# Unread products in TensorE's gaps, and the list of further passes made inside expert 0

## The chip, the cores and the metric

One Trainium2 chip, one core of it. The metric is the device time of one execution in microseconds (us), lower is better. TensorE is called PE below, VectorE DVE, ScalarE ACT, GpSimd POOL and SyncE SP.

## What is computed

One layer of a hybrid decoder trunk over 256 tokens of width 1024, in fp32. The last two thirds of it matter here: after the mixing sublayer a LayerNorm, a router that gives each token 4 of 32 experts, and the experts.

```python
x = layer_norm(ALPHA * x + mix, ln1_g, ln1_b)
logits = x @ w_router + b_router                 # (256, 32)
top_vals, top_idx = lax.top_k(logits, 4)         # gates = softmax(top_vals)
for e in range(32):
    g, u = split(x @ w_gate_up[e] + b_gate_up[e])    # 1024 -> 2 x 1024
    act = (clip(u, -7, 7) + 1) * (min(g, 7) * sigmoid(1.702 * min(g, 7)))
    out += combine[:, e] * (act @ w_down[e] + b_down[e])
h = ALPHA * x + out
x = layer_norm(h + sigmoid(h @ w_pg) * (p @ w_pp), ln2_g, ln2_b)
```

The kernel doesn't run every expert on every token. It gathers the tokens that chose the expert, up to 64 in a pass.

## The kernel before

The program writes out an order of instructions for each engine by hand, with semaphores between them (`wait_ge` before a step, `then_inc` behind it). There is no planner.

**Front** (to about 220 us). All weights come through one queue of transfers that SP issues, and PE takes the input projections, the attention, the convolution branch and the products of `mix` (L784 to L793).

**Between mix and the experts.** The residual is made in quarters on DVE (`residual`), turned on PE (`turn_res`, L795), copied out by ACT (`turned`), and multiplied with the router's weights on PE (`route`, L804). DVE picks the four experts of each token in `pick` (L1519 to L1537), which leaves a mask in `mask`, and raises `mask_ready` once for each half of the tokens. PE makes running counts with three small products (L832 to L834) and sums with twelve-odd tiny instructions (L837, L840). DVE forms each token's slot (L1561) and the one-hot matrix of experts 0 and 1 (`one_hot`, L461, `sel_ready`). PE gathers the rows of both experts with it: `gather` (L369 to L379), 16 products in two halves of 8, each two instructions of 128 columns, into banks 0 and 1. ACT copies each half out (L499).

**The list of further passes.** Behind the gather PE ranks the pairs of expert and pass that hold more than 128 tokens (L848, written to bank 7), DVE makes `place` from it (L1588), PE turns that into a list and its length (L850, L851), and DVE copies the list to integers (L1595, `more_out`). Only after this does PE wait for `wide_ready`, read the flag of expert 0 from SBUF into a register (`read_flag`, L511; the flag says if an expert has over 64 tokens) and branch on it. An expert with the flag 0 runs `one_round`, one with the flag 1 runs `two_rounds`. Here one expert, number 14, runs two rounds.

**one_round(e)** on PE (L962 to L987): turn the gates (L382), 32 products of the gathered rows with the gate and up weights (L388, 64 instructions), then turn the two sums (L395) once ACT has copied them (L1234). In expert 0 the first turning waits for `more_out`. Then the bias rows are turned (L944, expert 0 only), the expert before is combined (L408), in odd experts the next pair is gathered, and the down products follow (`use_down`, L388 again), which wait for `t_read`, raised by DVE's second addition at L434. DVE's part is `swiglu` (L428 to L452), ACT's the sigmoid (L457).

**Where the branches lie.** On PE the code of `one_round` follows in line and that of `two_rounds` stands behind everything. On ACT and DVE it is the other way: both wait for `wide_ready`, read the flag, and branch to `act_experts` or `dve_experts` past the code of all 32 `two_rounds` and of the further passes. On ACT this comes behind L499, on DVE behind L1595. DVE then reads the flag of the next expert before each `swiglu`.

**Weights.** Each expert takes 12 MB in six transfers of 2 MB. There are eleven slots for them. SP waits until a slot has been read (`chunk_used`, `gu_done`, `d_done`) before it issues the next transfer (L336 by the profile).

```python
                pe.wait_ge(more_ready, 1)                      # L847
                pe.matmul(bank[7][0:MORE, 1:2], upper[0:MORE, 0:MORE], need, ...).then_inc(rank_done, 1)
                pe.wait_ge(more_ready, 2)
                pe.matmul(bank[6][0:1, 3 * NE:3 * NE + LIST], expert_no, place, ...)
```

Of the kernel before, what the change touches and what calls it, by code (L numbers as in the profile page):

```python
# [7 lines left out]
D, S, P = 1024, 256, 128  # L8
# [21 lines left out]
NMORE = (S - WIDE) // CAP  # L30
MORE = NMORE * NE
LIST = NT * P * TOPE // CAP


Q0, K0, V0, QI0 = 0, 512, 1024, 1536
# [44 lines left out]
def program(nc, x, xT, pT, w_in, bT, bki, b_in, w_oa, w_oc, w_out, dwT, convT, ln1T, ln1g, ln1b, w_r, b_r,  # L80
# [4 lines left out]
    with ctx:  # L85
# [280 lines left out]
        def gate_bank(t, j):  # L366
            return bank[4 * t + j][:, 0:256]

        def gather(pe, b=4, first=False):  # L369

            for k in range(KD):
                if first and k % 4 == 0:
                    pe.wait_ge(x1_ready, 3 + k // 4)
                for t in range(NT):
                    mm = pe.matmul(bank[b + k // 4][:, (k % 4) * P:(k % 4 + 1) * P], x1_rows[:, t, k // 2, k % 2, :],  # L375
                                   sel[:, t, :, :], start=(t == 0), stop=(t == NT - 1))
                if k % 4 == 3:
                    mm.then_inc(gath_done, 1)
# [126 lines left out]
        def read_flag(eng, flag, e):  # L505
            if e == 1:
                eng.wait_ge(more_out, 1)
            eng.reg_load(flag, wide[0:1, e:e + 1] if e < NE else more[0:1, LIST:LIST + 1])

        with nc.Block() as block:  # L510
# [121 lines left out]
            def _(pe):  # L632
# [151 lines left out]
                def mix(t, j, ks=range(KD)):  # L784
                    for k in ks:
                        if t == 0 and k == 0:
                            wait_chunk(pe, 25 + j)
                        if t == 0 and j == 0:
                            pe.wait_ge(merged_ready, k + 1)
                        mm = pe.matmul(mix_bank(t, j), merged[:, k, t * P:(t + 1) * P], w_view(25 + j)[:, k, :],  # L790
                                       start=(k == 0), stop=(k == KD - 1))
                    if k == KD - 1 and (t == 1 or j == 3):
                        mm.then_inc(mix_done, 1)  # L793

                def turn_res(t, j):  # L795
                    pe.wait_ge(res_ready, 4 * t + j + 1)
                    if t == 1:
                        pe.wait_ge(rt_out, 3 + j)
                    for k in range(2):
                        mm = pe.transpose(turn_bank(t, j)[:, k * P:(k + 1) * P],  # L800
                                          res[:, t, (2 * j + k) * P:(2 * j + k + 1) * P], ident)
                    mm.then_inc(rt_done, 1)

                def route(t, ks):  # L804
                    for k in ks:
                        if k % 2 == 0:
                            pe.wait_ge(rt_out, 4 * t + k // 2 + 1)
                        mm = pe.matmul(bank[t][:, 0:NE], resT[:, k, t * P:(t + 1) * P], wr_sb[:, k, :],
                                       start=(k == 0), stop=(k == KD - 1))
                    if k == KD - 1:  # L810
                        mm.then_inc(rl_done, 1)
# [12 lines left out]
                turn_res(1, 2)  # L824
                route(1, range(4))
                mix(1, 3, range(4, KD))
                route(1, range(4, 6))
                turn_res(1, 3)
                route(1, range(6, KD))

                pe.wait_ge(mask_ready, 2)
                pe.matmul(bank[6][:, 0:NE], upper, mask[:, 0, 0:NE], start=True, stop=True)  # L832
# [5 lines left out]
                for j in range(NMORE):  # L838
                    for t in range(NT):
                        mm = pe.matmul(bank[7][j * NE:(j + 1) * NE, 0:1], mask[:, t, 0:NE], ones[:, 0:1],  # L840
                                       start=(t == 0), stop=(t == NT - 1))
                mm.then_inc(cum_done, 1)

                pe.wait_ge(sel_ready, 1)
                gather(pe, 0, True)

                pe.wait_ge(more_ready, 1)  # L847
                pe.matmul(bank[7][0:MORE, 1:2], upper[0:MORE, 0:MORE], need, start=True, stop=True).then_inc(rank_done, 1)  # L848
                pe.wait_ge(more_ready, 2)
                pe.matmul(bank[6][0:1, 3 * NE:3 * NE + LIST], expert_no, place, start=True, stop=True)  # L850
                pe.matmul(bank[6][0:1, 3 * NE + LIST:3 * NE + LIST + 1], need, ones[0:MORE, 0:1], start=True, stop=True  # L851
                          ).then_inc(list_done, 1)

                top = nc.cur_bb
                flag = pe.alloc_register("pe_two_rounds")

                def pair(n):
                    pe.wait_ge(e_in[slot_no[n]], filled[n])  # L860
# [102 lines left out]
                def one_round(e):  # L963
                    q = e % 2
                    weights = lambda c: pair(load_no(e, c))
                    turn_gates(pe, selg[:, q]).then_inc(sgt_done, 3)
                    embedded(e)
                    use_gate_up(e, q, weights, e == 0)
                    for j, (rows, to) in enumerate(((h_gate, gate_turned), (h_up, up_turned))):
                        pe.wait_ge(h_out, 4 * e + 1 + j)  # L970
                        if j:
                            pe.wait_ge(g2_out, 3 * e + 3)
                        elif e:
                            pe.wait_ge(rows_out, 2 * e)
                        else:
                            pe.wait_ge(more_out, 1)
                        turn(pe, rows, to).then_inc(t_done, 1 + 2 * j)
                    read_flag(pe, flag, e + 1)
                    if e == 0:
                        turn_bias(gate_sum)  # L980
                    before(e)
                    if q == 1 and e < NE - 1:
                        next_gather(e)
                    if e in (PP_E, PP_E + 2):
                        embed(e)
                    use_down(e, weights)

                def two_rounds(e):
                    q = e % 2
                    weights = lambda c: pair(load_no(e, c))  # L990
                    turn_gates(pe, selg[:, q]).then_inc(sgt_done, 1)
                    embedded(e)
                    if e == 0:
                        pe.wait_ge(more_out, 1)
                        turn_bias(gate_turned)
                        pe.wait_ge(xt_ready, 1)
                    pe.wait_ge(selb_ready, 3 * e + 1)
                    for k in range(KD):
                        for t in range(NT):
                            mm = pe.matmul(gate_sum[:, k * CAP:(k + 1) * CAP], x1_rows[:, t, k // 2, k % 2, :],  # L1000
                                           sel_b[:, t, :], start=(t == 0), stop=(t == NT - 1))
                    mm.then_inc(sgt_done, 1)
                    pe.wait_ge(g2_out, 3 * e + 2)
                    if e:
                        pe.wait_ge(rows_out, 2 * e)
                    else:
                        pe.wait_ge(bias_ready, 1)
                    use_gate_up_twice(e, q, weights)
                    read_flag(pe, flag, e + 1)
                    before(e)  # L1010
                    for j, (rows, to) in enumerate(((h_gate, gate_sum), (h_up, up_sum))):
                        pe.wait_ge(h_out, 4 * e + 1 + j)
                        turn(pe, rows, to).then_inc(t_done, 1)
                    for j, (rows, to) in enumerate(((h_gate, gate_turned), (h_up, up_turned))):
                        pe.wait_ge(h_out, 4 * e + 3 + j)
                        turn(pe, rows, to).then_inc(t_done, 1)
                    pe.wait_ge(t_read, 2 * e + 1)
                    pe.wait_ge(selb_ready, 3 * e + 3)
                    for t in range(NT):
                        mm = pe.transpose(gate_sum[:, t * P:(t + 1) * P],  # L1020
                                          selg[:, q, t].rearrange("p h c -> p (h c)"), ident)
                    mm.then_inc(sgt_done, 1)
                    if q == 1 and e < NE - 1:
                        pe.wait_ge(g2_out, 3 * e + 3)
                        next_gather(e)
                    use_down_twice(e, weights)
                    pe.wait_ge(rows_out, 2 * e + 1)
                    pe.wait_ge(g2_out, 3 * e + 3)
                    combine(pe, 1 - q).then_inc(d_done, 1)
                    if e in (PP_E, PP_E + 2):  # L1030
                        embed(e)

                pe.wait_ge(wide_ready, 2)
                read_flag(pe, flag, 0)
                for e in range(NE):
                    if e % 2 == 0:
                        if e:
# [294 lines left out]
            def _(v):  # L1332
# [227 lines left out]
                for t in range(NT):  # L1560
# [24 lines left out]
                gates_by_slot(v, 0, 1)  # L1585
                v.wait_ge(more_ready, 1)
                v.wait_ge(rank_done, 1)
                nc.vector.tensor_scalar(place, iota_e[0:MORE, 0:LIST], bank[7][0:MORE, 1:2], need, ALU.is_equal, ALU.mult  # L1588
                                        ).then_inc(more_ready, 1)
                v.wait_ge(zeroed, 1)  # L1590
                nc.vector.tensor_copy(gate_rows.rearrange("p t (h c) -> p t h c", h=2)[:, :, :, 0:NE],
# [135 lines left out]
```

## Time and profile before

| | |
|---|---|
| time, median of 3 runs | 1195.64 us (1194.48 to 1196.38) |
| the profiled execution: time, span | 1196.13 us, 1194.4 us |
| PE, DVE, ACT busy | 97%, 25%, 14% |
| DMA, mean over the span | 375 GB/s, 448.16 MB |

The span is what the profiler saw, and the time has 1.7 us around it. "Busy" counts an engine's data instructions alone. PE instructions overlap, so a group's busy time is shorter than its count times the duration of one. PEclk is the clock that TensorE was granted: 1.00 is 2.4 GHz, 0.50 is 1.2 GHz. Durations of weight loads (PEld) lie beside the products.

### The profile page before, as it was taken

Reading aid. Unit: us, or ns where it says so; the run is one execution under the profiler, and the core shown is the slowest. Engines: PE = TensorE matmul, PEld = TensorE weight load, DVE = VectorE, ACT = ScalarE, POOL = GpSimd, SP = SyncE. Lnnn points to the kernel's source line nnn. Section 1 sums busy time; section 2 is a strip of 40 time slices with the busy share of each in tenths; the row PEclk is TensorE's granted clock in tenths of the full one; section 3 lists DMA queues with packets and bytes.
Section 4 is the critical chain, followed back from the end, with each engine's and each line's share of the span. In section 5 each row is a group of like instructions: output and inputs, shape, how many; then the busy total and the mean of one; then the engine's idle time right before and its main releaser. Section 6 shows DMA issues by size and latency. Waiting matters only on the chain.

```text
span 1194.4 us, 13688 instructions
## 1 busy us (share of the span) xinstructions
PE 1153.3 (97%) x5606; PEld 580.7 (49%) x5606; DVE 297.1 (25%) x769; ACT 172.5 (14%) x335; POOL 11.5 (1%) x26
## 2 busy tenths in 40 slices
PE   7999999899999999999999799999999999999997
PEld 6888888834343434434343343434343343434346
DVE  0549932611111121111110211111112111111125
ACT  1204130111010111101010111101111111111112
POOL 0020000000000000000000000000000000000000
PEclk9999999899999999999998899999999999999999
DMA  9994466779999999999999999999999999999980
GB/s 324 346 292 141 141 254 239 276 325 426 427 427 427 428 427 427 428 426 428 428 424 427 395 364 421 427 429 427 428 427 426 430 426 427 425 428 428 428 347 36
DMA packets 64887, 448.16 MB, mean 375 GB/s; under 512 B 7120, under 2 KB 36080, under 8 KB 39984
## 3 DMA queue, kind: packets, MB, share of 16 engines
q1 hardware_dynamic: 58352, 440.84, 89.7%
q10 hardware_dynamic: 6464, 6.33, 1.6%
q8 instruction: 49, 0.80, 0.3%
q14 instruction: 22, 0.18, 0.0%
HBM read 444.53 MB, written 2.62 MB: 374 GB/s over the span
## 4 chain that ended last, share of the span: by engine, by line
PE 89%; DVE 4%; DMA 4%; ACT 1%; issue 1%; ACTq 0%; DVEq 0%
PE bank L388 56%; PE bank L648 11%; PE bank L375 5%; DMA ring<-in_w_gu 3%; PE bank L408 3%; PE bank L777 2%; PE bank L790 2%; PE bank L1066 2%; PE bank L395 2%; PE bank L703 1%; DVE arena L434 1%; PE bank L382 1%; DVE arena L428 1%; ACT arena L1234 1%; DVE arena L452 1%
## 5 line engine op out<-in xcount | busy, mean ns | idle before, releaser
L388 PE MATMUL bank<-ring,arena 128*64 128x512 f32 x1712 | 379.2, 597 | 9.8 <-issue 5.2
L388 PE MATMUL bank<-arena 128*64 128x512 f32 x1456 | 322.9, 597 | 4.6 <-DVE arena L434 3.9
L388 PEld LDWEIGHTS bank<-ring,arena 128*64 128x64 f32 x1712 | 120.6, 137 | 246.3 <-issue 231.9
L388 PEld LDWEIGHTS bank<-arena 128*64 128x64 f32 x1456 | 102.1, 138 | 207.8 <-issue 194.1
L428 DVE TENSOR_TENSOR arena<-bank,arena 128x512 f32<-128x512 f32 x33 | 22.8, 692 | 614.1 <-PE bank L395 614.1
L648 PE MATMUL bank<-arena,ring 128*128 128x256 f32 x576 | 129.0, 385 | 0.0
L648 PEld LDWEIGHTS bank<-arena,ring 128*128 128x128 f32 x576 | 110.6, 193 | 17.4 <-issue 2.2
L1234 ACT ACTIVATE arena<-bank 128x512 f32<-128x512 f32 x62 | 37.1, 598 | 396.2 <-PE bank L388 396.2
L408 PE MATMUL bank<-arena 64*128 64x512 f32 x272 | 67.6, 615 | 2.0 <-ACT arena L1237 1.4
L375 PEld LDWEIGHTS bank<-sel,arena 128*128 128x128 f32 x512 | 63.5, 202 | 11.8 <-issue 11.4
L375 PE MATMUL bank<-sel,arena 128*128 128x128 f32 x512 | 66.6, 290 | 0.3 <-DVE sel L461 0.3
L1237 ACT ACTIVATE arena<-bank 128x512 f32<-128x512 f32 x33 | 19.7, 597 | 249.5 <-PE bank L388 247.4
L395 PEld LDWEIGHTS bank<-arena 128*128 128x128 f32 x264 | 36.7, 209 | 35.0 <-issue 25.9
L395 PE MATMUL bank<-arena 128*128 128x128 f32 x264 | 48.8, 309 | 3.1 <-ACT arena L1234 0.4
L1420 DVE SCALAR_TENSOR_TENSOR arena<-arena 128x256 f32<-128x256 f32 x120 | 48.5, 477 | 0.7 <-DVE arena L1420 0.2
L408 PEld LDWEIGHTS bank<-arena 64*128 64x128 f32 x272 | 23.5, 186 | 24.4 <-issue 17.5
L461 DVE TENSOR_TENSOR sel<-arena 128x256 f32<-128x256 f32 x16 | 6.8, 425 | 108.9 <-PE bank L382 108.8
L1132 ACT ACTIVATE arena<-bank,arena 128x256 f32<-128x256 f32 x36 | 16.8, 473 | 103.0 <-PE bank L648 103.0
L452 DVE TENSOR_TENSOR arena<-arena 128x256 f32<-128x256 f32 x66 | 28.1, 425 | 5.0 <-ACT arena L457 1.1
L499 ACT ACTIVATE arena<-bank 128x512 f32<-128x512 f32 x32 | 19.1, 597 | 70.2 <-PE bank L375 70.2
L448 DVE SCALAR_TENSOR_TENSOR arena<-arena 128x256 f32<-128x256 f32 x66 | 28.0, 425 | 4.2 <-DVE arena L444 0.3
L790 PE MATMUL bank<-ring,arena 128*128 128x256 f32 x128 | 28.4, 380 | 0.0
(196 smaller groups left out, 529.7 us busy)
## 6 DMA issues: line engine op xcount, KB each, us to landing
ring<-in_w_gu SPq DMA_DIRECT2D x70, 2048.0 KB, 25.7
arena<-in_w_gu SPq DMA_DIRECT2D x58, 2048.0 KB, 27.2
ring<-in_w_dn SPq DMA_DIRECT2D x35, 2048.0 KB, 25.0
arena<-in_w_dn SPq DMA_DIRECT2D x29, 2048.0 KB, 26.6
ring<-in_w_in SPq DMA_DIRECT2D x19, 1024.0 KB, 12.6
ring<-in_w_out SPq DMA_DIRECT2D x4, 1024.0 KB, 5.6
arena<-in_w_pg SPq DMA_DIRECT2D x2, 2048.0 KB, 44.2
ring<-in_w_oa SPq DMA_DIRECT2D x2, 1024.0 KB, 5.7
```

The lines of the kernel that those rows point to most:

```text
L375: mm = pe.matmul(bank[b + k // 4][:, (k % 4) * P:(k % 4 + 1) * P], x1_rows[:, t, k // 2, k % 2, :], sel[:, t, :, :], start=(t == 0), stop= ...
L388: mm = pe.matmul(to[half * CAP:(half + 1) * CAP, :], rows, w[:, half * 512:(half + 1) * 512], start=first, stop=last)
L395: mm = pe.transpose(to[:, j * P:(j + 1) * P], blocks[:, j, :], ident)
L408: mm = pe.matmul(total[t][n][:, :], G2[a:a + CAP, q, t * P:(t + 1) * P], ysb[a:a + CAP, :], start=first, stop=last)
L428: nc.vector.tensor_tensor(by_bias(gt, 8), by_bias(of_gate[:, :], 8), bias_of(e, 0, 0, 8), ALU.add).then_inc(sw_step, 1)
L448: nc.vector.scalar_tensor_tensor(up[:, at], up[:, at], 1.0, gt[:, at], ALU.add, ALU.mult).then_inc(sw_step, 1 + 6 * skip * j)
L452: nc.vector.tensor_tensor(to[:, at], up[:, at], sg[:, at], ALU.mult).then_inc(act_ready, 1 + 2 * skip * j)
L648: mm = pe.matmul(bank[n % 4][:, 0:S], w[:, k, j * P:(j + 1) * P], xT_sb[:, k, :], start=(k == 0), stop=(k == KD - 1))
L777: mm = pe.matmul(bank[n % 4][:, 0:S], w_view(i)[:, k, (c % 4) * P:(c % 4 + 1) * P], rhs[:, k, :], start=(k == 0), stop=(k == 3))
L790: mm = pe.matmul(mix_bank(t, j), merged[:, k, t * P:(t + 1) * P], w_view(25 + j)[:, k, :], start=(k == 0), stop=(k == KD - 1))
L1234: a.activation(rows, of[:, :], ACT.Identity).then_inc(h_out, 1 + 2 * j)
L1420: nc.vector.scalar_tensor_tensor(cy[:, a, :], u_sb[:, a, bass.ds(j, S)], dw[:, a, bass.ds(j, 1)], cy[:, a, :], ALU.mult, ALU.add).then_inc ...
```

## The change

Five unread products of 256 columns (`keep_clock`) are put where PE waits: one behind the last turning of the residual, three behind the last route product, one behind the counts. They write bank 0, which the gather overwrites. The gather is split in two, and the wait for `wide_ready` and the reading of expert 0's flag go between the halves. The rank product writes bank 6 in place of bank 7. The two list products leave the place ahead of expert 0 and follow the gate and up products of expert 0 (the copy at L1595 so follows there too, and the turning behind them still waits for it). The wait and flag reading ahead of the loop over the experts go.

```diff
+RANK = 3 * NE + LIST + 1
@@ gather
-        def gather(pe, b=4, first=False):
-            for k in range(KD):
+        def gather(pe, b=4, first=False, ks=range(KD)):
+            for k in ks:
@@ tensor, between mix and the gather
+                def keep_clock(n):
+                    for _ in range(n):
+                        pe.matmul(bank[0][:, 0:S], ident, resT[:, 0, :], start=True, stop=True)
                 route(1, range(4, 6))
                 turn_res(1, 3)
+                keep_clock(1)
                 route(1, range(6, KD))
+                pe.wait_ge(mask_ready, 1)
+                keep_clock(3)
 
                 pe.wait_ge(mask_ready, 2)
                 pe.matmul(bank[6][:, 0:NE], upper, mask[:, 0, 0:NE], start=True, stop=True)
...
                 mm.then_inc(cum_done, 1)
+                keep_clock(1)
 
                 pe.wait_ge(sel_ready, 1)
-                gather(pe, 0, True)
-
+                gather(pe, 0, True, range(4))
+                flag = pe.alloc_register("pe_two_rounds")
+                pe.wait_ge(wide_ready, 2)
+                read_flag(pe, flag, 0)
+                gather(pe, 0, True, range(4, KD))
                 pe.wait_ge(more_ready, 1)
-                pe.matmul(bank[7][0:MORE, 1:2], upper[0:MORE, 0:MORE], need, start=True, stop=True).then_inc(rank_done, 1)
-                pe.wait_ge(more_ready, 2)
-                pe.matmul(bank[6][0:1, 3 * NE:3 * NE + LIST], expert_no, place, start=True, stop=True)
-                pe.matmul(bank[6][0:1, 3 * NE + LIST:3 * NE + LIST + 1], need, ones[0:MORE, 0:1], start=True, stop=True
-                          ).then_inc(list_done, 1)
+                pe.matmul(bank[6][0:MORE, RANK:RANK + 1], upper[0:MORE, 0:MORE], need, start=True, stop=True
+                          ).then_inc(rank_done, 1)
                 top = nc.cur_bb
-                flag = pe.alloc_register("pe_two_rounds")
+                def list_further():
+                    pe.wait_ge(more_ready, 2)
+                    pe.matmul(bank[6][0:1, 3 * NE:3 * NE + LIST], expert_no, place, start=True, stop=True)
+                    pe.matmul(bank[6][0:1, 3 * NE + LIST:3 * NE + LIST + 1], need, ones[0:MORE, 0:1], start=True,
+                              stop=True).then_inc(list_done, 1)
@@ one_round
                     use_gate_up(e, q, weights, e == 0)
+                    if e == 0:
+                        list_further()
@@ two_rounds
                     if e == 0:
+                        list_further()
                         pe.wait_ge(more_out, 1)
@@ ahead of the loop over experts
-                pe.wait_ge(wide_ready, 2)
-                read_flag(pe, flag, 0)
                 for e in range(NE):
@@ vector
-                nc.vector.tensor_scalar(place, iota_e[0:MORE, 0:LIST], bank[7][0:MORE, 1:2], need, ALU.is_equal, ALU.mult
+                nc.vector.tensor_scalar(place, iota_e[0:MORE, 0:LIST], bank[6][0:MORE, RANK:RANK + 1], need, ALU.is_equal, ALU.mult
```

## Rows read from the trace of the kernel before

**Rows 1.** Windows: each stretch, busy time of PE, granted clock, DMA share, GB/s
```profile
234.00:238.00 4.00, 4.00 (x20) 4.00 (x21) 3.06 (x13) 0.41 (x1) 0.81 (x2) 0.50 1.00 426
...
240.00:242.00 2.00, 1.03 (x9) 0.53 (x10) 0.58 (x3) 0.44 (x1) 0.00 (x0) 1.00 0.04 12
...
687.00:689.00 2.00, 1.31 (x7) 0.69 (x8) 0.00 (x0) 0.60 (x1) 0.00 (x0) 1.00 0.77 172
```

**Rows 2.** Waits of PE, 690 to 1194 us: total, times, longest
```profile
PE bank L388 <- DMA ring<-in_w_gu: 0.5, 1, 0.5
```

**Rows 3.** Chain that ended last, 225 to 262 us: start, length, what
```profile
231.44 0.64 PE bank L832 x2
...
232.50 0.44 PE bank L834 x2
...
233.77 6.03 PE bank L375 x32
239.80 0.22 PE bank L848 x2
...
240.46 0.20 PE bank L850 x2
...
240.70 0.51 issue
...
241.64 13.91 PE bank L388 x64
```

**Rows 4.** Timeline, 222 to 241 us: start, busy, engine, line, count, [idle before <-releaser]
```profile
222.88 1.89 PE L790 MATMUL bank<-ring,arena 128*128 128x256 f32 x8
...
225.02 0.98 PE L808 MATMUL bank<-wr_sb,arena 128*128 128x32 f32 x8
...
229.24 0.63 PE L808 MATMUL bank<-wr_sb,arena 128*128 128x32 f32 x4 [0.47 <-ACT arena L1209]
...
235.29 0.28 DVE L1573 CAST wide<-arena 1x32 int32<-1x32 f32 x1
...
240.74 0.17 DVE L1595 CAST more<-bank 1x17 int32<-1x17 f32 x1 [0.20 <-PE bank L851]
```

**Rows 5.** Chain that ended last, a later gather
```profile
285.29 3.97 PE bank L375 x32
```

**Rows 6.** Timeline of expert 0, 253 to 261 us
```profile
256.24 0.69 DVE L428 TENSOR_TENSOR arena<-bank,arena 128x512 f32<-128x512 f32 x1 [15.34 <-PE bank L395]
...
257.81 1.99 PE L408 MATMUL bank<-arena 64*128 64x512 f32 x8 [0.56 <-ACT arena L1245]
...
260.52 5.80 PE L388 MATMUL bank<-ring,arena 128*64 128x512 f32 x26 [0.73 <-DVE arena L434]
```

**Rows 7.** Timeline of ACT, 232 to 262 us, around its branch to the experts
```profile
239.84 0.60 ACT L499 ACTIVATE arena<-bank 128x512 f32<-128x512 f32 x1 [1.66 <-PE bank L375]
243.05 0.38 ACT L1229 ACTIVATE arena<-bank 128x256 f32<-128x256 f32 x1 [2.62 <-issue]
```

**Rows 8.** DMA queues, 240 to 244 us: packets, MB, share of 16 engines
```profile
q14 instruction: 3, 0.02, 2.0%
```

**Rows 9.** Timeline, 596 to 675 us: expert 13's DVE work, then expert 14
```profile
606.45 0.69 DVE L428 TENSOR_TENSOR arena<-bank,arena 128x512 f32<-128x512 f32 x1 [13.21 <-PE bank L395]
...
609.24 0.41 DVE L434 TENSOR_TENSOR arena<-bank,arena 128x256 f32<-128x256 f32 x1
...
620.24 0.60 ACT L1237 ACTIVATE arena<-bank 128x512 f32<-128x512 f32 x1 [6.49 <-PE bank L388]
622.01 0.44 PE L382 MATMUL bank<-arena 128*128 128x128 f32 x2 [1.88 <-issue]
...
625.56 0.38 ACT L1229 ACTIVATE arena<-bank 128x256 f32<-128x256 f32 x1 [4.72 <-issue]
```

**Rows 10.** Windows of PE, expert 14's wait and what follows: clock third from the end
```profile
670.50:671.00 0.50, 0.00 (x0) 0.50 1.08 459
```

**Rows 11.** Timeline of PE, 655 to 695 us: the products behind that wait
```profile
671.00 16.00 PE L388 MATMUL bank<-ring,arena 128*64 128x512 f32 x64 [5.20 <-issue]
```

## The prediction

> **What bounds the kernel now.** I read the granted clock over the span first, then the waits of PE and the share of the DMA engines, then the chain between 225 and 262 us, and last the timelines of ACT and DVE there. The clock is 1.00 but for a few stretches. One of them covers all of 234 to 238 us, where it is 0.50 (1.2 GHz) [rows 1]. Ahead of it PE had only 0.63 us of small router products and then stood idle until 231.44 us [rows 3, 4]. From there on the chain is PE's and DVE's in turn: counts, one-hot, gather, rank, list, flag, first expert [rows 3].
>
> The experts are close to both limits, PE and the transfers. What matters is which clock sets their end. The transfers have no work at 240 to 242 us (share 0.04), because all slots are full, and again they slacken behind expert 14 (0.77 at 687 to 689 us) [rows 1]. Both times PE frees the slots that restart them. Behind that PE waits for a transfer once, 0.5 us [rows 2]. So the end moves with PE's time at expert 14: what PE gains up to the down products of expert 0 arrives at the end in full, and a stream of weights that merely begins earlier gives nothing.
>
> **The parts and their costs.** All times are against the profiled execution, 1196.13 us around a span of 1194.4. That is 0.49 above the median, and I apply the difference to the median of 1195.64.
>
> *Unread products.* A product of 256 columns is two instructions. Eight such instructions take 1.89 us at the full clock [rows 4], so about 0.43 us a product with the pipeline's end taken off. The first falls into the 0.47 us that PE waits for ACT at 229.24 us [rows 4]. Three behind the last router product add 1.3 us from about 229.6 and end near 231.0, before the mask at 231.44 [rows 3]: nothing on the path. Bounds: 0 if they fit, 0.4 us if the last runs over. I take 0. The fifth starts behind the counts and ends about when the one-hot is there, again 0 (up to 0.4). None of them issues a transfer, and no queue but PE's is touched.
>
> *What the clock gives back.* The stretch would look like the one at 222 to 226 us, where small router products alternate with products of 256 columns and the clock stayed at full [rows 4]. The three count products take 0.44 us each at half clock [rows 3], and four router products take 0.98 us at full [rows 4], 0.25 each. The counts end near 232.3 in place of 232.94. DVE has ended its work before them by then, so it takes them up at once: 0.64 us. The gather takes 6.03 us [rows 3] and a later one of the same 32 instructions 3.97 [rows 5]: 2.06 us. Together 2.7; if the clock falls as before, 0, less 0.4 for the fifth product at half clock.
>
> *Flag between the halves.* `wide_ready` comes at 235.57, 1.8 us behind the gather's start [rows 3, 4], and the first half takes 2.0, so the wait is covered. The reading itself has no row of its own. From below it is 0: the same reading stands between L395 and L944 or L408 in expert 0 with no gap. From above it is the 0.51 us of "issue" in front of L382, which holds this reading, a wait and a branch [rows 3]. I take half, 0.25. If it is dear, half of that gap is what is bought with it, so the sum hardly changes.
>
> *Rank, list, flag out of the way.* From the rank product (239.80) to the gates' turning (241.21) are 1.41 us (0.51 of "issue" from 240.70 ends there) [rows 3]. Left are the rank's instructions and a branch, 0.2 and 0.25: 1.0 us gained. The turning needs bank 7 alone, and the rank is now in bank 6, so it doesn't wait for DVE.
>
> Sum at the start of expert 0's products: 2.7 - 0.25 + 1.0 = 3.45 us earlier.
>
> *List inside expert 0.* Its two products follow the last of the 64 instructions, at 255.5 by the times of before (241.64 + 13.91) [rows 3]. L850 began 0.28 us before L1595, which takes 0.17 [rows 3, 4], so `more_out` comes near 255.95 and the gate's turning is up to 0.5 us late. On PE alone 0.3 to 0.5 us would be lost, since the up sum is turned only at 256.28 anyway.
>
> **The new wait.** L1595 is queued on DVE ahead of its flag reading, its branch to the experts, a second flag reading and all of `swiglu`. Before, they had 15.34 us of idle time to hide in [rows 6]. Now the first addition wants to start at 256.2 to 256.8, and L1595 is issued at 255.75. ACT shows what the same sequence costs (wait, reading, branch past 32 two-round blocks): 3.21 us from the start of L499 to the start of L1229, with nothing but "issue" in between [rows 7], and instruction packets in the DMA queues there [rows 8]. That was with the weight queue silent. In expert 14, with the queue full, ACT's far branch took 4.72 us behind L1237, and PE's left 1.88 us of idle time that its backlog didn't cover [rows 9]. Expert 0 has the full queue too. Bounds for DVE from issue to first addition: 0.4 (nothing but readings) and 5.3 (ACT in expert 14, from 620.24). I take 4.3, ACT's quiet 3.2 plus about 1 for the loaded queue and the second reading: first addition at 260.05.
>
> The Trainium skill says in "Runtime: NRT & Kernel Launch", section "Instruction fetch mechanics", that a taken branch beyond the fetched window waits for a transfer of the target page. The trace agrees with it by the 2.62 us and the packets [rows 7, 8].
>
> From DVE's first addition to the end of its second L434, which releases the down products, are 3.20 us where the sigmoid's table is loaded [rows 9]. So the down products start near 263.3, against 260.52 [rows 6]: 2.85 us late. Net gain 3.45 - 2.85 = 0.6 us.
>
> **The rivals.**
>
> *A, the branch is cheap (0.21).* If DVE's readings and branches take under a microsecond, only the 0.3 to 0.5 us of the late turning are lost, and the gain is 3.1: 1192.5. For it: expert to expert the branches leave no gap. Against it: the 2.62 and 4.72 us, both at far targets. The Trainium skill, "Advanced Engine Details and Errata", section "Control Flow Timing", puts a branch at about 51 ns and a compare-and-branch at about 108 ns, which is this rival's case; the sum by it would be A's.
>
> *B, the clock falls all the same (0.14).* The gap of about 0.4 us before the mask and the small counts behind it may be thin enough. Then the 2.7 us stay away, the fifth product runs at half clock into the gather (0.4), and with DVE's 2.85 the sum is -0.4 - 0.25 + 1.0 - 2.85: 2.5 us slower, 1198.1. It decides against the change as soon as DVE's delay exceeds 0.4 us. Against it: the filled stretch has only gaps under half a microsecond.
>
> *C, the clock falls inside expert 0 (0.22).* PE would idle from about 260.1, where L408 ends [rows 6], to 263.3. In expert 14 the clock fell in an idle time of 5.20 us [rows 10, 11], and the 64 instructions behind it took 16.00 in place of 13.91 [rows 3, 11]: 2.1 us. Net 1.5 slower: 1197.1. For it: 3.2 us are twice the gap in which the clock fell at 231 us. Against it: dense products stand directly on both sides.
>
> *D, the products don't fit or the flag's wait stalls the gather (0.05).* Some 0.5 to 1 us off the gain, near 1195.8.
>
> **How the numbers follow.** The forecast, DVE late and both clocks held, has 0.38: 1195.64 - 0.6 = 1195.0. Its own range, with DVE's sequence from 3.2 to 5.3 us, is 1193.8 to 1196.0. A measurement of this kernel tells about 0.2% from no change, 2.4 us, so the bounds are 1193.2 and 1198.0. Faster has nearly all of A and a little of the forecast with a quick branch: 0.22. Slower has most of B and the bad end of C: 0.13. The rest, 0.65, is neither. The range reaches from A's middle to B's lower part: 1192.4 to 1197.8.
>
> **What would show it.** In the changed kernel's profile the clock should be 1.00 through 228 to 240 us, and the first gather some 4.2 us long. L382 should follow the rank product within 0.5 us, with the gates' turning near 237.8. In expert 0 the two list products should stand behind the 64, with L1595 0.3 us later, and DVE's first addition behind an idle time ended by "issue", 4 us after L1595, with instruction packets in between. PE's down products should wait there for DVE's L434 for over 3 us. DVE's addition within a microsecond of L1595 would make the forecast wrong towards A, a clock of 0.50 in either stretch towards B or C. So would any wait of PE for a transfer between experts 0 and 14, since then PE's gain wouldn't reach the end.

## The result and the profile after

The changed kernel takes 1201.07 us (median of 20 runs, 1196.39 to 1203.23) against 1195.89 (20 runs, 1193.89 to 1196.80) for the kernel before: ratio 1.0044, 95% interval 1.0037 to 1.0051, so 5.2 us slower. It lies above the forecast of 1195.0 us and above the range, which ended at 1197.8. The profiled execution has 1199.94 us and a span of 1198.2, 3.8 us over the profile before.

The timeline of the changed kernel from 225 to 268 us, lines left out (line numbers behind L369 move by 1, those of PE's and DVE's late parts by up to 19; L831 are the unread products):

```profile
229.91 1.54 PE L831 MATMUL bank<-arena 128*128 128x256 f32 x6
231.65 0.41 PE L841 MATMUL bank<-arena 128*128 128x32 f32 x2 [0.20 <-DVE arena L1551]
...
232.77 0.70 PE L831 MATMUL bank<-arena 128*128 128x256 f32 x2
...
233.34 2.15 PE L376 MATMUL bank<-sel,arena 128*128 128x128 f32 x16
...
235.73 2.12 PE L376 MATMUL bank<-sel,arena 128*128 128x128 f32 x16 [0.23 <-issue]
...
237.98 0.44 PE L383 MATMUL bank<-arena 128*128 128x128 f32 x2
...
238.35 13.95 PE L389 MATMUL bank<-ring,arena 128*64 128x512 f32 x64
...
252.51 0.16 DVE L1612 CAST more<-bank 1x17 int32<-1x17 f32 x1 [13.92 <-PE bank L872]
...
252.82 1.21 PE L396 MATMUL bank<-arena 128*128 128x128 f32 x8 [0.35 <-DVE more L1612]
...
259.34 0.69 DVE L429 TENSOR_TENSOR arena<-bank,arena 128x512 f32<-128x512 f32 x1 [6.67 <-issue]
...
260.65 1.28 ACT L458 ACT_TABLE_LOAD   x1 [5.99 <-DVE arena L431]
...
263.02 0.42 DVE L435 TENSOR_TENSOR arena<-bank,arena 128x256 f32<-128x256 f32 x1
```

PE's timeline of the changed kernel, 262 to 300 us:

```profile
263.49 9.76 PE L389 MATMUL bank<-ring,arena 128*64 128x512 f32 x32 [6.70 <-DVE arena L435]
273.18 0.44 PE L383 MATMUL bank<-arena 128*128 128x128 f32 x2
```

The same two lines of the kernel before, PE's timeline, 256 to 285 us:

```profile
260.52 7.09 PE L388 MATMUL bank<-ring,arena 128*64 128x512 f32 x32 [0.73 <-DVE arena L434]
267.54 0.44 PE L382 MATMUL bank<-arena 128*128 128x128 f32 x2
```

The first half reads as forecast. The two halves of the gather take 2.15 and 2.12 us where the whole took 6.03 [rows 3], the flag costs 0.23 us between them, and the products of expert 0 start at 238.35 in place of 241.57: 3.2 us earlier (3.45 forecast). The second half is where the time goes. DVE copies the list at 252.51 and adds the first bias at 259.34, with 6.67 us of "issue" in between, PE stands idle for 6.70 us, and the down products start at 263.49, 3.0 us later than before. Then they take 9.76 us in place of 7.09. The windows of the changed kernel (busy time of each engine, granted clock, DMA share, GB/s) say why:

```profile
258.00:260.00 2.00, 0.00 (x0) 0.00 (x0) 0.66 (x1) 0.00 (x0) 0.00 (x0) 1.00 1.02 434
260.00:262.00 2.00, 0.00 (x0) 0.00 (x0) 1.52 (x5) 1.34 (x2) 0.00 (x0) 1.00 0.99 426
262.00:263.50 1.50, 0.01 (x2) 0.01 (x2) 0.79 (x3) 0.57 (x1) 0.00 (x0) 0.53 0.83 344
263.50:266.00 2.50, 2.50 (x6) 0.75 (x8) 1.11 (x3) 0.00 (x0) 0.00 (x0) 0.50 0.09 39
266.00:268.00 2.00, 2.00 (x8) 0.65 (x6) 0.00 (x0) 0.00 (x0) 0.00 (x0) 0.50 0.00 0
268.00:270.00 2.00, 2.00 (x10) 0.56 (x8) 0.00 (x0) 0.00 (x0) 0.00 (x0) 0.77 0.00 0
```

The clock fell to 0.50 (1.2 GHz) behind some five idle microseconds of PE. So expert 1 begins (L383) at 273.18, against 267.54 before: 5.6 us late. The weights also stop for some 6 us (share 0.09 and less from 263.5 to 270 us): SP sends the next ones only when a slot has been read, and the late down products free none before. The later part differs by the clock in expert 14. The changed kernel's timeline there:

```profile
627.73 0.44 PE L383 MATMUL bank<-arena 128*128 128x128 f32 x2 [1.93 <-issue]
628.55 5.35 PE L1019 MATMUL bank<-arena 128*128 128x64 f32 x32 [0.39 <-DVE arena L484]
634.58 29.14 PE L389 MATMUL bank<-arena 128*64 128x512 f32 x128 [0.69 <-ACT arena L1289]
675.13 15.62 PE L389 MATMUL bank<-ring,arena 128*64 128x512 f32 x64 [5.21 <-issue]
```

And the kernel before, PE's timeline, 612 to 700 us:

```profile
622.83 6.20 PE L1000 MATMUL bank<-arena 128*128 128x64 f32 x32 [0.38 <-DVE arena L483]
629.72 29.89 PE L388 MATMUL bank<-arena 128*64 128x512 f32 x128 [0.69 <-ACT arena L1272]
```

The changed kernel's turning is 5.7 us late and the products behind the long wait 4.1 us [rows 9, 11]: the same instructions take 5.35 and 29.14 us where they took 6.20 and 29.89, because more of this thin stretch (small products with short waits) ran at the full clock. That is luck of this one execution. Without its 1.5 us the profiles would differ by 5.3 us and not 3.8, close to the 5.2 of the medians and the 5.6 at the start of expert 1.

### The profile page after: what moved, and what is told of

Same layout as the page of the kernel before. It is cut to its first block, busy times and chain, and to the rows that moved or that the text cites. A ratio compares the mean times of both kernels' runs of the same rounds, so it can differ in the third digit from the quotient of the medians.

```text
span 1198.2 us, 13708 instructions
## 1 busy us (share of the span) xinstructions
PE 1153.2 (96%) x5616; PEld 578.7 (48%) x5616; DVE 297.5 (25%) x769; ACT 172.7 (14%) x335; POOL 11.5 (1%) x26
## 4 chain that ended last, share of the span: by engine, by line
PE 88%; DVE 4%; DMA 4%; issue 2%; ACT 1%; DVEq 0%; ACTq 0%
PE bank L389 56%; PE bank L649 11%; PE bank L376 5%; DMA ring<-in_w_gu 3%; PE bank L409 3%; PE bank L778 2%; PE bank L791 2%; PE bank L1083 2%; PE bank L396 2%; PE bank L704 1%; DVE arena L435 1%; DVE arena L429 1%; PE bank L383 1%; ACT arena L1251 1%; DVE arena L453 1%
```

## The experiments

Unless it says otherwise, each starts from the changed kernel. Ratios are to the kernel before, run on the same chip.

### e1_list_back: the list products ahead of expert 0 again

```diff
-                    if e == 0:
-                        list_further()
...
+                list_further()
                 def pair(n):
```

> The list products go back ahead of expert 0; the unread products, the split gather and the flag between its halves stay. Theory (DVE's flag reading and far branch, uncovered behind the late list copy, are the whole loss): DVE's first addition again has an idle time ended by PE, the clock stays 1.00 to expert 14, and the products of expert 0 start about 2.6 us earlier than before, so the time is 1193.2, 2.7 us under the kernel before. Rival (the unread products or the flag between the halves cost something the profile does not show): at or above 1196. Rival (the early gain does not reach the end): within 0.5 us of before.

1193.61 us, ratio 0.9974 (0.9960 to 0.9988): 3.1 us under before by the ratio. The whole loss is gone with the place of the list. Unread products and split gather cost nothing that shows.

### e2_list_alone: the late list, and nothing else of the change

```diff
-                keep_clock(1)
...
-                pe.wait_ge(mask_ready, 1)
-                keep_clock(3)
...
-                keep_clock(1)
...
-                gather(pe, 0, True, range(4))
-                gather(pe, 0, True, range(4, KD))
+                gather(pe, 0, True)
...
+                pe.wait_ge(wide_ready, 2)
+                read_flag(pe, flag, 0)
                 for e in range(NE):
```

> The list products in expert 0 alone; no unread products, one whole gather, the flag read ahead of the loop as before. Theory: only the rank, list and copy time of about 0.7 us is gained ahead of expert 0, and 6 to 9 us are lost in it (late first addition, table load, half clock), so about 1203, 7 us over the kernel before and 2 us over the changed one. Rival (the late list costs only the 0.3 to 0.5 us of the late turning, and the rest of the loss comes with the unread products): 1195.5.

The rank product stays in bank 6 as well. 1202.25 us, ratio 1.0055 (1.0040 to 1.0070), 6.6 us slower. Its timeline shows the same 6.8 us:

```profile
253.05 0.17 DVE L1607 CAST more<-bank 1x17 int32<-1x17 f32 x1 [13.93 <-PE bank L864]
...
259.98 0.69 DVE L429 TENSOR_TENSOR arena<-bank,arena 128x512 f32<-128x512 f32 x1 [6.77 <-issue]
```

The rival that put most of the loss on the unread products falls. Expert 0's products start at 238.89 us, 2.7 us ahead of before where 0.7 were expected. Of this 0.9 us is there already at the first count product (230.54 against 231.44), so it has nothing to do with the edit, and 0.5 us is a shorter gather (5.52 us in place of 6.03, as the clock came back earlier).

### e3_list_early: the list products near the start of expert 0

```diff
                     for k in range(KD - 2):
+                        if wait_xt and k == 2:
+                            list_further()
                         if k % 2 == 0:
...
-                    if e == 0:
-                        list_further()
```

> The changed kernel with the two list products between the second and third eighth of expert 0's gate and up products, 2 us behind their start, in place of behind the last. Theory (the place of the list decides, because DVE's copy, flag reading and far branch need 7 us of cover): cover is 12 us, DVE's first addition follows its turning at once, expert 0's down products start 3.2 us earlier than before, time 1192.7. Rival (the branch costs PE or the weights something wherever it lies): above 1195. Rival (the list in the middle of the sums breaks PE's run): 0.4 us more than the theory.

1194.65 us, ratio 0.9981 (0.9966 to 0.9996). DVE is in time:

```profile
241.99 0.17 DVE L1612 CAST more<-bank 1x17 int32<-1x17 f32 x1 [3.63 <-PE bank L872]
...
253.12 0.69 DVE L429 TENSOR_TENSOR arena<-bank,arena 128x512 f32<-128x512 f32 x1 [10.96 <-PE bank L396]
...
257.40 4.94 PE L389 MATMUL bank<-ring,arena 128*64 128x512 f32 x22 [0.73 <-DVE arena L435]
```

The down products start 3.1 us before those of the kernel before, as expected, but the time is 1.0 us lower by the medians and 2.3 by the ratio. In its profile 3.3 us of lead are still there at the products behind expert 14's long wait (667.67 against 671.00). Its waits of PE for transfers, total, times, longest, name what ate a part of them (before: 0.5 us in all [rows 2]):

```profile
PE bank L389 <- DMA ring<-in_w_gu: 2.2, 2, 1.2
```

### e4_branch_first: DVE branches first, then copies the list

```diff
-                v.wait_ge(list_done, 1)
-                nc.vector.tensor_copy(more[:, :], ...).then_inc(more_out, 1)
...
                 def one_round(e):
+                    copy_list(e)          # the two lines above, for e == 0
                     next_pair(e)
```

> The changed kernel, list products behind the last product as there, but DVE reads its flag and branches to the experts first and copies the list in expert 0's own code. Theory (the far branch is what is late, not the copy): DVE's first addition comes within 1 us of the list copy, the down products start about 2.7 us earlier than before, time 1193.2. Rival (the late copy itself, by PE's wait on it and the late turnings, costs the time): no better than 1199.

1195.21 us, ratio 0.9993 (0.9984 to 1.0002).

```profile
252.68 0.17 DVE L1620 CAST more<-bank 1x17 int32<-1x17 f32 x1 [13.92 <-PE bank L872]
...
253.75 0.69 DVE L429 TENSOR_TENSOR arena<-bank,arena 128x512 f32<-128x512 f32 x1 [0.90 <-PE bank L396]
```

The copy is as late as in the changed kernel and is followed by the addition after 1.07 us in place of 6.83. The median is 5.9 us lower. So what was late in the changed kernel was what stands there between copy and addition: flag reading and branch.

### e5_dve_near: the same order, a near target

```diff
                 read_flag(v, flag, 0)
-                v.br("dve_experts")
-                for e in range(NE):
-                    nc.switch_bb(f"dve_two_rounds{e}", parent=top)
-                    two_rounds(e)
...
-                nc.switch_bb("dve_experts", parent=top)
                 for e in range(NE):
                     v.br_ne(flag, 0, f"dve_two_rounds{e}", f"dve_one_round{e}")
...
+                v.br("dve_end")
+                for e in range(NE):
+                    nc.switch_bb(f"dve_two_rounds{e}", parent=top)
+                    two_rounds(e)
```

> The changed kernel with DVE's code laid out as PE's is: one_round in line behind the flag reading, two_rounds and the further passes behind everything, so that the branch into expert 0 has a near target. Nothing else differs. Theory (the far target and the fetch of its code make DVE late): DVE's first addition comes within 1.5 us of the list copy in place of 6.8, the clock stays at 1.00 in expert 0, and the time falls from 1201 to about 1195. Rival (two flag readings and any branch cost it, near or far): still 5 us or more behind the copy, time near 1201.

1193.65 us, ratio 0.9989 (0.9977 to 1.0000).

```profile
251.28 0.17 DVE L1612 CAST more<-bank 1x17 int32<-1x17 f32 x1 [13.92 <-PE bank L872]
...
252.35 0.69 DVE L429 TENSOR_TENSOR arena<-bank,arena 128x512 f32<-128x512 f32 x1 [0.91 <-PE bank L396]
```

Both flag readings and a conditional branch are still there, and the interval is 1.07 us. The far target makes the other 5.8. The profiled execution took only 1189.7 us: PE's thin stretch in expert 14 ran at the full clock (1.00 from 600 to 640 us, 0.87 before), so the median is the number to use.

### e6_quiet: no weights on their way while DVE branches

```diff
+                sp.wait_ge(sw_step, 1)
                 for n in range(ES, NG):
                     sp.wait_ge(*pair_read(last_in[n]))
```

> The changed kernel, but no weights are sent for again until DVE's first addition of expert 0, so DVE's far branch meets idle DMA engines. A look at one interval: list copy to first addition. Theory (the fetch waits behind the weights' transfers): 3.2 to 3.6 us, as ACT's in the quiet stretch, in place of 6.8. Rival (the fetch takes 6 to 7 us whatever else moves): 6 or more. The total is meant to be worse, by up to 10 us, since the weights restart late.

```profile
251.45 0.17 DVE L1613 CAST more<-bank 1x17 int32<-1x17 f32 x1 [13.92 <-PE bank L873]
...
255.35 0.69 DVE L429 TENSOR_TENSOR arena<-bank,arena 128x512 f32<-128x512 f32 x1 [3.74 <-issue]
```

3.90 us from copy to addition, 0.3 above the expected bound and 2.9 under the 6.83 with the weights moving. The DMA share was 0.02 or less from 250 to 256 us. So in this one execution (1204.44 us, worse because the weights restart late) the far branch costs some 3 us over e5's 1.07 by itself, and behind a full queue of weights 3 more.

### e7_fill_expert0: the clock held through the gap

```diff
                     before(e)
+                    if e == 0:
+                        for _ in range(14):
+                            pe.matmul(up_sum[:, 0:S], ident, x1[:, 0, 0:S], start=True, stop=True)
```

> The changed kernel with 14 unread products of 256 columns (6.0 us) in PE's gap ahead of expert 0's down products. DVE is as late as there. Theory (the half clock behind the gap is a part of the loss by itself): clock 1.00 throughout expert 0, its down products back to 7.1 us from 9.8, time about 1198.4, 2.7 us under the changed kernel. Rival (the clock in expert 0 doesn't matter): 1201.

```profile
259.06 0.69 DVE L429 TENSOR_TENSOR arena<-bank,arena 128x512 f32<-128x512 f32 x1 [6.66 <-issue]
...
263.19 7.09 PE L389 MATMUL bank<-ring,arena 128*64 128x512 f32 x32 [0.44 <-DVE arena L435]
270.21 0.44 PE L383 MATMUL bank<-arena 128*128 128x128 f32 x2
```

DVE is as late, the down products take 7.09 us in place of 9.76, and expert 1 starts 3.0 us earlier than in the changed kernel. The time is 1200.38 us (5 runs), ratio 1.0039 (1.0026 to 1.0052): 0.7 us under the changed kernel where 2.7 were expected. In its profile PE waits 2.4 us for weights near the end. The half clock's price is shown at the start of expert 1, and what of it arrives at the end isn't settled by this run.

### e8_early_no_fill: e3 without the five unread products

e3, and of it:

```diff
-                keep_clock(1)
...
-                pe.wait_ge(mask_ready, 1)
-                keep_clock(3)
...
-                keep_clock(1)
```

> The list products early in expert 0 and the flag between the halves, without the five unread products. Theory (the unread products hold the clock and are worth 2.7 us at the start of expert 0, of which about 1 us reaches the end because the last experts then wait for weights): the clock is 0.50 over most of the gather, expert 0's products start 0.5 us earlier than before, time 1195.5, 0 to 1 us above the same kernel with them. Rival (all of it reaches the end): 1197.3. Rival (the clock held without them in many runs): 1194.6.

```profile
233.38 5.69 PE L376 MATMUL bank<-sel,arena 128*128 128x128 f32 x32 [0.35 <-DVE sel L462]
...
239.58 3.65 PE L389 MATMUL bank<-ring,arena 128*64 128x512 f32 x16
```

1194.66 us, ratio 0.9991 (0.9980 to 1.0001). The gather is slow again and expert 0's products start 1.4 us later than e3's, though still 2.0 us ahead of before (0.5 expected). The medians don't differ (1194.65 and 1194.66); by the ratios it is 1.2 us, inside the intervals. The clock does what was said of it, but that the unread products make the kernel faster isn't shown.

### e9 to e11: PE made late on purpose

All start from e3. The edit is that of e9, with expert 0 and 14 products for e10, and expert 0 and 5 products for e11:

```diff
                     before(e)
+                    if e == 24:
+                        for _ in range(5):
+                            pe.matmul(up_sum[:, 0:S], ident, x1[:, 0, 0:S], start=True, stop=True)
```

> e3_list_early with 5 unread products in expert 24 ahead of its down products: PE is 1.6 us later there (2.15 us less the 0.56 us gap that is there). Theory (what PE wins ahead of expert 0 is partly spent at the end, waiting for weights, 2.2 us in the profile of e3): the wait shrinks by what PE is late, time up by 0.5 us at most, 1194.7 to 1195.2. Rival (PE sets the end): up by 1.6 us, 1196.3.

> e3_list_early with 14 unread products (6.0 us) ahead of expert 0's down products: PE 5.3 us later there, DVE in time, clock 1.00. The down products then start 0.5 us before those of e7_fill_expert0. Theory (only the time at which expert 0's down products start counts, not how it came about): 1199.9, 0.5 us under e7. Rival (a DVE branch that meets the weights costs more than PE's wait in expert 0): 1198 or less.

> e3_list_early with 5 unread products (2.15 us) ahead of expert 0's down products: PE 1.4 us later there and still 1.7 us ahead of the kernel before. Theory (the first 2 us or so of PE's lead are spent waiting for weights at the end): up by 0.7 us at most, 1195.3 or less. Rival (PE's lead reaches the end in full): up by 1.4 us, 1196.1.

e9: 1195.22 us, ratio 0.9989 (0.9978 to 1.0001), 0.6 us over e3 by the medians and 1.0 by the ratios: inconclusive. e10: 1199.21, ratio 1.0035 (1.0022 to 1.0048), 0.7 us under the expected 1199.9 and within the interval of e7. Within the noise of five runs each, PE late by its own work costs what PE late by DVE costs, so no hidden price of the branch shows. e11: 1196.23, ratio 1.0001 (0.9989 to 1.0013), 1.6 us over e3 by the medians and 2.4 by the ratios, with 1.4 us of work added. That is nearer the rival's 1.4 than the theory's 0.7 at most, but the intervals of e3 and e11 overlap, so that the lead is lost in full is likely and not shown.

### e12_early_near: e3 in the layout of e5

```diff
+                        if wait_xt and k == 2:
+                            list_further()
...
-                    if e == 0:
-                        list_further()
...
-                v.br("dve_experts")
...
+                v.br("dve_end")
+                for e in range(NE):
+                    nc.switch_bb(f"dve_two_rounds{e}", parent=top)
```

> e3_list_early with DVE's code in the near layout of e5_dve_near: both covers at once. Theory: DVE is in time in either case, so nothing is added, 1193.7 to 1194.7. Rival (fewer far fetches of code leave the weights' transfers faster): 1192 or less.

1194.28 us, ratio 0.9985 (0.9973 to 0.9998). As the theory has it: nothing is added to what e3 or e5 has alone.

### e13 to e15: the weights taken away as a limit

```diff
-            sp.dma_start(slot_of(n), pair_source(e, c)).then_inc(e_in[slot_no[n]], 16)
+            if n < ES or type(e) is not int:
+                sp.dma_start(slot_of(n), pair_source(e, c)).then_inc(e_in[slot_no[n]], 16)
+            else:
+                sp.dma_start(slot_of(n)[:, 0:3 * PAIR // 4], pair_source(e, c)[:, 0:3 * PAIR // 4]).then_inc(...)
```

This stands in the kernel before (e13), in the changed one (e14) and in e3 (e15). These kernels leave out a quarter of each later transfer, so their outputs aren't those of the layer, and only their times are of use.

> The kernel before, sending only three quarters of each expert's weight transfer from the twelfth on; the products run over the whole slot, so the experts' outputs are of partly stale weights. PE's work is unchanged. Both theories: no wait for weights, 0.5 us under the kernel before or up to 2 us where runs waited longer: about 1194.5.

> The changed kernel with three quarters of each weight transfer from the twelfth on, as in e13. DVE's late branch and the half clock in expert 0 stay. Theory (PE's loss in expert 0 is the loss of the change): 5 us over e13. Rival (part of the changed kernel's loss was weights that restarted late): 3 us or less over e13.

> e3_list_early with three quarters of each weight transfer from the twelfth on, as in e13. Theory (weights at the end took part of the lead): with them out of the way the lead of 3.2 us arrives, 3 us under e13. Rival (the lead gets lost elsewhere, with the clock in expert 14): 1 to 1.5 us under e13, as e3 against before.

e13 1188.71 us (ratio 0.9950, 0.9937 to 0.9963), e14 1193.98 (0.9988, 0.9979 to 0.9997), e15 1186.85 (0.9929, 0.9916 to 0.9942). The changed kernel stays 5.3 us over its counterpart by the medians and 4.5 by the ratios, as the theory has it and not the rival's 3 or less, so its loss is PE's in expert 0 and not one of weights. DVE needs 7.66 us from copy to first addition there, with a DMA share of 0.94 to 1.00 from 252 to 260 us. The early list is 1.9 us under by the medians and 2.5 by the ratios, nearer the theory's 3 than the rival's 1 to 1.5 by the latter and between the two by the former, with intervals of 1.5 us each. That e13 itself falls by 6.9 us was expected by neither. Its timeline in expert 14:

```profile
618.74 0.44 PE L385 MATMUL bank<-arena 128*128 128x128 f32 x2
...
624.23 27.69 PE L391 MATMUL bank<-arena 128*64 128x512 f32 x128 [0.69 <-ACT arena L1275]
...
663.31 15.51 PE L391 MATMUL bank<-ring,arena 128*64 128x512 f32 x64 [5.20 <-issue]
```

The 1.88 us of "issue" in front of PE's turning [rows 9] are gone: with less traffic PE's own far branch is covered. And from that turning to the products behind the long wait expert 14 takes 44.57 us in place of 48.99, because the clock stayed at 1.00 (0.87 in the mean from 600 to 640 us before).

## Why the prediction was wrong

**The gain ahead of expert 0: right.** Unread products cost nothing on the path, the clock stayed at 1.00, the gather took 4.5 us with the flag in it (4.2 forecast), the turning followed the rank product at 237.98 (237.8 forecast). The start of expert 0's products moved by 3.2 us, 3.45 forecast. The part of the unread products in it is at the upper end, though. From the first count product to the rank product the profile of before takes 8.29 us and the changed kernel's 6.13, but the three other profiles without unread products take 7.78 (e2), 7.95 (e8) and 7.84 (e13). So they are worth 1.7 to 2.2 us there with the flag's price taken off, where the prediction had 2.45. The flag costs 0.23 us here, but 0.7 in the profiles of e9 and e14, where the second half of the gather waits for `wide`.

**The new wait: the mechanism was right, its size was not.** This is the step that failed. The prediction gave DVE's flag reading, far branch and second reading 4.3 us from the start of the list copy, with 5.3 as the upper bound. They take 6.83 us in the changed kernel, 6.93 in e2, 6.84 in e7 and 7.66 in e14. Of the 4.3 the quiet part, ACT's 3.21 us [rows 7], was near: e6 gives 3.90, with the second reading in it. What was mis-sized is the term for the full queue and the second reading, put at about 1 us. It is 3.6 us, 2.9 of them the full queue (6.83 against 3.90). The 5.3 was no bound: it came from ACT in expert 14, which reads no flag there (it has read it in expert 13), while DVE in expert 0 reads two. If the readings make the difference between the two engines isn't shown. e4 and e5 show that neither copy nor readings but the far target is the cost: 1.07 us without it.

**The chain behind it: 1 us short.** From the first addition to the down products 3.20 us were taken from expert 13. There the sigmoid's table is in place already, and ACT loads nothing. Expert 0 needs 4.15, because ACT loads the table first (1.28 us, at 260.65). The prediction put this load at nothing without a reason, and rows of its own had the right size: expert 0 before took 4.28 us, from 256.24 to 260.52 [rows 6]. The load doesn't run ahead of the wait either. In the changed kernel, e2, e4 and e5 it begins right behind DVE's clipped sum (L431). Before, it seemed to start by itself behind L1245, because that sum (L430) was just done by then. The router's table load is another case: at 229.59 us in the changed kernel it begins 2 us ahead of its activation. Why the two differ isn't shown.

**Rival C happened on top.** With 6.7 us of idle time and not 3.2, the fall of the clock in expert 0, given 0.22 and 2.1 us, came about and cost 2.7 at the start of expert 1. Together: 3.2 gained, then 6.2 lost in DVE's wait and 2.7 in the clock, 5.6 us net at the start of expert 1. How much of the 2.7 is in the 5.2 us of the whole is open, since e7 takes the half clock away and the time falls by 0.7 us.

**The side was missed through a rival of the wrong place.** The slower side was given 0.13, most of it for a clock that falls before the gather (B). That did not happen. What decides is DVE's delay itself, once it exceeds the 3.2 us gained, and more so when it lets the clock fall. That had no share in the slower side except through C.

**That PE's gain reaches the end in full: not confirmed.** The kernels with DVE in time have their down products 2.6 to 4.0 us earlier than before (e1, e3, e4, e5, e12) and medians 0.5 to 2.1 us lower. Two things scatter by as much between executions: the clock in expert 14 (from expert 1's turning to the products behind the long wait the same work takes 401.95 us in the changed kernel's profile, 403.46 in that of before, 399.32 in e5's and 405.21 in e9's) and waits for weights in the last two experts, 0.5 us in the profiles of before and after, 2.2 in e3's, none in e9's. e7, which is late, has 2.4 us of them, so they don't come from the lead alone. These two are all there is in the profiles: from the start of the products behind expert 14's long wait to the end of the span, the fourteen profiles with all weights take 522.6 to 523.5 us plus these waits (e9's 1.6 us of added work taken off). So a lead that is still there at expert 14 arrives, less the waits for weights. e15 against e13 is 1.9 to 2.5 us faster with a lead of 1.5 us between their profiles in expert 0's down products (257.68 against 259.21; the lead is 3.1 between e3 and before). What brings the waits about, and how much of the lead they take on the average, stays open.

The best version run is e1, with the list where it was: 0.9974 (0.9960 to 0.9988) of the time before. e3 and e12 are below the kernel before too, with intervals that overlap with e1's.

## What to carry to other kernels

When an instruction is moved later, look at what stands behind it on its engine's queue, control flow included: a flag reading and a far branch that had hidden in 15 us of idle time made the longest wait that PE has (6.70 us). Price a far branch at the load that the DMA engines have there, not where they are quiet, or keep the usual path in line. And where a wait can grow beyond the idle time at which TensorE's clock has been seen to fall, add the half clock to the wait's price.

## What had not been expected of the hardware

A far branch on DVE, with its flag readings, takes 3.9 us from the start of the instruction ahead of it to the first one behind with no weights moving (e6, one profile). In the four profiles where it meets the weights it takes 6.8 to 7.7 us, 6.83 of them at 427 GB/s in the changed kernel. There one packet for code shows between 256 and 257 us, over 4 us behind the copy, and the addition comes at least 2.3 us later. The DMA queues, 256 to 257 us:

```profile
q14 instruction: 1, 0.01, 1.9%
```

The Trainium skill, "Runtime: NRT & Kernel Launch", section "Instruction fetch mechanics", has the mechanism (a taken branch beyond the fetched window waits for a transfer of its target). The trace agrees in that a packet for code lies in the gap, and e5, with the near target, has none from 250 to 254 us. What passes in the 4 us ahead of the packet isn't shown.

Taking a quarter of the weights away made the kernel before 6.9 us faster (e13), though in the profile of before PE waits only 0.5 us for weights. That isn't all a price of the full queue. Between the two profiles, whose spans differ by 8.9 us, 1.3 us lie ahead of expert 0's products, 1.9 in PE's own far branch into expert 14 (1.88 us of idle time with the full load, none without), 4.4 in the clock inside expert 14 and 1.2 behind it. The clock can hold there under the full load too: e5's profile has the same 44.57 us for that stretch, and e15's, with the light load, 47.45. If the light load makes it hold more often isn't shown.
